# Scans of a hybrid recurrent layer: the next chunk's level matrices earlier, read-outs side by side, the second attention in two parts, the pairs behind the fourth level

## The reference, cut to what matters

```python
def step(S, inp):                       # RWKV-7, 6 heads of 64, one token after the other
    r_t, w_t, kk_t, a_t, v_t, k_t = inp
    sa = jnp.einsum('dbhij,dbhj->dbhi', S, -kk_t)
    S = S * w_t[..., None, :] + sa[..., None] * (kk_t * a_t)[..., None, :] + v_t[..., None] * k_t[..., None, :]
    return S, jnp.einsum('dbhij,dbhj->dbhi', S, r_t)

def step(S, inp):                       # GLA, 4 heads, chunks of 64 tokens
    qc, kc, vc, lac = inp
    b = jnp.cumsum(lac, axis=2)
    diff = b[:, :, :, None] - b[:, :, None, :]
    dec = jnp.exp(jnp.where(mask, diff, -jnp.inf))
    att = jnp.einsum('dbthk,dbshk,dbtshk->dbhts', qc, kc, dec)
    o = jnp.einsum('dbhts,dbshv->dbthv', att, vc) + jnp.einsum('dbthk,dbhkv->dbthv', qc * jnp.exp(b), S)
    bl = b[:, :, -1]
    S = S * jnp.exp(bl)[..., None] + jnp.einsum('dbshk,dbshv->dbhkv', kc * jnp.exp(bl[:, :, None] - b), vc)
    return S, o
```

## Time and profile before

| | |
|---|---|
| runs | 3509.75, 3511.60, 3511.67 us; median 3511.6 |
| profiled execution | 3508.28 us, its span 3506.5 us |
| busy share of the span | PE 90%, DVE 65%, ACT 46%, POOL 25% |
| stage of the scans, 965.0 to 1772.2 us | 807.2 us; PE busy 761.0, DVE 633.4, ACT 386.7, POOL 509.0 |
| one chunk, 1403.04 to 1426.02 us | 22.98 us; PE busy 21.90, DVE 18.48, ACT 11.31, POOL 15.08 |

### The profile page before, as it was taken

How to read it: one execution, slowest core, us unless ns; L and a number is a source line. 1 busy time by engine, 2 the same in 40 slices (tenths; PEclk the granted TensorE clock), 3 DMA queues, 4 the chain that set the end, 5 groups by cost and what they waited for, 6 DMA issues and landing times. The chain is left out here.

```text
span 3506.5 us, 90832 instructions
## 1 busy us (share of the span) xinstructions
PE 3151.4 (90%) x37105; PEld 2875.5 (82%) x37105; DVE 2283.7 (65%) x4484; ACT 1617.0 (46%) x2917; POOL 873.0 (25%) x1232
## 2 busy tenths in 40 slices
PE   7899989999689999999959981799999999999996
PEld 3887867777489889999947760699999999999996
DVE  4575549995478778778867768455555555555555
ACT  2313756665445445444446540344444444444454
POOL 0110000000066666666622200111121111111213
PEclk8999999999799999999979985799999999999998
DMA  5465336665644554444356632565566555655685
GB/s 177 126 182 172 85 99 197 201 201 156 179 109 103 130 135 102 107 106 98 79 155 193 179 105 96 170 194 181 182 200 203 188 189 185 193 181 184 205 291 186
DMA packets 583428, 561.43 MB, mean 160 GB/s; under 512 B 211550, under 2 KB 527262, under 8 KB 582138
## 3 DMA queue, kind: packets, MB, share of 16 engines
q1 hardware_dynamic: 547084, 447.27, 42.7%
q0 software_dynamic: 36016, 109.52, 10.6%
HBM read 418.33 MB, written 138.33 MB: 159 GB/s over the span
## 5 line engine op out<-in xcount | busy, mean ns | idle before, releaser
L3431 DVE TENSOR_TENSOR exp_wlo<-exp_raw,exp_whi 128x2048 fp32r<-128x2048 f32 x192 | 440.0, 2293 | 364.1 <-ACT exp_whi L3332 356.5
L3332 ACT CAST exp_whi<-exp_raw 128x2048 fp32r<-128x2048 f32 x189 | 360.1, 1905 | 75.0 <-DMA exp_raw<-in_w_up 73.5
L1030 PE MATMUL mix_acc<-proj_hThi,mix_wlo 128*128 128x448 f32 (+3 forms) x920 | 357.8, 389 | 14.5 <-DVE mix_wlo L1398 14.5
L1030 PE MATMUL mix_acc<-proj_hTlo,mix_whi 128*128 128x448 f32 (+3 forms) x920 | 335.9, 365 | 0.0
L1030 PE MATMUL mix_acc<-proj_hThi,mix_whi 128*128 128x448 f32 (+3 forms) x920 | 335.7, 365 | 0.0
L3261 PE MATMUL moe_o<-moe_hidhi,exp_wlo 128*128 128x272 f32 x1024 | 308.3, 301 | 2.6 <-DVE moe_hidlo L3545 2.6
L3261 PE MATMUL moe_g<-moe_xThi,exp_wlo 128*128 128x272 f32 x1024 | 300.4, 293 | 1.0 <-DVE moe_xTlo L3435 1.0
L3261 PE MATMUL moe_o<-moe_hidhi,exp_whi 128*128 128x272 f32 x1024 | 298.4, 291 | 0.0
L3261 PE MATMUL moe_g<-moe_xThi,exp_whi 128*128 128x272 f32 x1024 | 297.6, 291 | 0.0
L3261 PE MATMUL moe_u<-moe_xThi,exp_wlo 128*128 128x272 f32 x1024 | 297.1, 290 | 0.0
L3261 PE MATMUL moe_u<-moe_xThi,exp_whi 128*128 128x272 f32 x1024 | 296.9, 290 | 0.0
(11 more groups left out here) (391 smaller groups left out, 8557.9 us busy)
## 6 DMA issues: line engine op xcount, KB each, us to landing
exp_raw<-in_w_gate SPq DMA_DIRECT2D x64, 1024.0 KB, 5.1
exp_raw<-in_w_up SPq DMA_DIRECT2D x64, 1024.0 KB, 5.1
exp_raw<-in_w_down SPq DMA_DIRECT2D x64, 1024.0 KB, 5.1
scn_plain<-rec SPq DMA_DIRECT2D x68, 384.0 KB, 3.6
rec<-mix_arena SPq DMA_DIRECT2D x24, 896.0 KB, 4.3
proj<-mix_out POOLq DMA_DIRECT2D x88, 224.0 KB, 2.5
scn_grc<-grec SPq DMA_DIRECT2D x136, 128.0 KB, 3.7
mix_arena<-in_w_ada SPq DMA_DIRECT2D x12, 1024.0 KB, 6.3
```

The lines of the kernel that those rows point to most:

```text
L1030: mm = pe.matmul(acc[n % ACCS][0:width, 0:tn], wt[:, k, 0:width], hT[hp][:, k, t0:t0 + tn], start=k == 0 and i == 0, stop=k == KD - 1 and ...
L3332: act.copy(w[k % RING][0][:, :, :], raw[k % RAW][:, :, :]).then_inc(hi_done[k % RING], 1)
L3431: dve.tensor_tensor(w[k % RING][1][:, :, :], raw[k % RAW][:, :, :], w[k % RING][0][:, :, :], ALU.subtract).then_inc(lo_done[k % RING], 1)
```

## The change

`attention` gets the range of levels that it is to issue, and `chunk` of PE and of DVE are put in another order. No arithmetic is added or removed. Lines that are the same on both sides are cut.

```diff
-                def attention(g, c):
+                def attention(g, c, levels):
                     u = c % NB
-                    for e in (bk_done if g == 0 else kT_done):
-                        pe.wait_ge(e, c + 1)
-                    if g:
+                    if levels.start == 0:
+                        for e in (bk_done if g == 0 else kT_done):
+                            pe.wait_ge(e, c + 1)
+                        pe.wait_ge(kf_done[g], c + 1)
+                        pe.wait_ge(qf_done[g], c + 1)
+                    if g and levels.stop == NA:
                         pe.wait_ge(lm_done[1], min(c + 2, NCH))
-                    pe.wait_ge(kf_done[g], c + 1)
-                    pe.wait_ge(qf_done[g], c + 1)
-                    for l in range(NA):
+                    for l in levels:
...
# PE, chunk(c)
                     joined(c, 1)
...
+                    if c + 1 < NCH:
+                        strict(c + 1)
                     values_seen(c)
+                    grown(c, 1)
                     read_out(0, c)
-                    grown(c, 1)
                     read_out(1, c)
                     joined(c, 2)
                     state_seen(c)
                     grown(c, 2)
                     keys_by_token(c)
-                    if c + 1 < NCH:
-                        strict(c + 1)
                     joined(c, 3)
                     keys_turned(c)
                     grown(c, 3)
-                    attention(0, c)
+                    attention(0, c, range(NA))
                     joined(c, 4)
+                    attention(1, c, range(CA))
                     grown(c, 4)
-                    attention(1, c)
+                    attention(1, c, range(CA, NA))
                     joined(c, 5)
                     gla_added(0, c)
+                    grown(c, 5)
                     old_state_out(0, c)
-                    grown(c, 5)
                     corrected(0, c)
...
# DVE, chunk(c)
                     joined(c, 1)
...
+                    if more:
+                        strict(0, c + 1)
                     values_seen(0, c)
                     values_seen(1, c)
                     turned(c, 1)
                     read_out(0, c)
                     read_out(1, c)
                     joined(c, 2)
+                    if more:
+                        strict(1, c + 1)
                     turned(c, 2)
                     joined(c, 3)
-                    if more:
-                        strict(0, c + 1)
                     turned(c, 3)
-                    if more:
-                        strict(1, c + 1)
-                        pairs(0, c + 1)
                     joined(c, 4)
+                    attention_masked(0, c)
                     turned(c, 4)
                     if more:
-                        pairs(1, c + 1)
-                    attention_masked(0, c)
+                        pairs(0, c + 1)
                     joined(c, 5)
                     attention_summed(0, c)
+                    if more:
+                        pairs(1, c + 1)
                     attention_masked(1, c)
```

## The result

The changed kernel takes 3551.62 us (median of four runs, 3547.21 to 3556.91), the kernel before in the same comparison 3511.64 (3509.75 to 3513.39): a ratio of 1.0115, 95% interval 1.0099 to 1.0131. The forecast was 3490, 3472 to 3504, with 7 in 100 for slower. It was wrong in sign, and the time lies 48 us above the top of the range.

What follows compares the result with a forecast made beforehand. PE's list, dense but for holes such as 0.93 us before `grown` 4, was taken to bound each scan chunk; 35.3 + 0.3 - 3.9 - 12.4 + 1.5 = 20.8 us saved gave 3490 us, range 3472 to 3504.

Steps and rivals of the forecast that it cites:

- the last stretch on DVE: DVE from the fourth `Ys` to the end of the last masking: 6.73 us where it was 6.35, mask ending at 18.77.
- The slow rival: Early `strict` or its mask slips beyond a 0.3 us margin, delaying the second `joined`: some 3522 us; chance 0.08.
- The holes ahead of `grown` 4 and in front of the mask: PE's 0.93 us wait before level 4's `grown` goes; a new 0.7 us hole comes before the second `old_state_out`.
- 21.9: Length in us forecast for an undisturbed chunk, down from 22.98, 1.07 less.
- The switch to wide loads: PE's read-outs side by side go in and out of 128-column loads once: 0.31 us less per chunk.
- The first chunk: PE's early `strict` waits for the second chunk's load, landing at 973.75: 3.9 us lost.
- The hidden delays of 12.4 us: PE's own holes, formerly hidden in the wait for `Ys` before `grown` 4, now cost 12.4 us; bounds 0 and 12.4.
- 12.4 less 1.5: Cost of newly exposed PE delays, less 1.5 us won back where the new 0.7 hole hides delays before `corrected`.
- The sum of 20.8 us: Total gain over the scans: 35.3 + 0.3 - 3.9 - 12.4 + 1.5 = 20.8 us.
- 35.3 + 0.3 - 3.9: 33 chunks shorter by 1.07 us each, the last chunk's switch gain, less the first chunk's wait for the load.
- The chances: Whole-kernel odds: faster (under 3504.6 us) 0.84, same 0.09, slower 0.07.
- the rivals: Delays stay hidden (3478) 0.22; gain handed back behind level four (3507 to 3515) 0.2; slower 0.08; forecast itself 0.5.

Runs made afterwards that it cites:

- the run with `strict` alone: Kernel before with only strict(c + 1) of PE and DVE moved to the start of the chunk: ratio 0.9970, 3501.1 us.
- the held run: Changed kernel plus one POOL wait: its first large product of group 0 waits for DVE's last sum of the chunk before; ratio 0.9946, 3492.6 us.
- The kernel before with the wait on POOL: Kernel before plus a wait of POOL's first large product of group 0 for DVE's last sum of the chunk before: ratio 0.9993.

## Why the prediction was wrong, by its steps

- **The step that failed: the last stretch on DVE.** It said that from `Ys` 4 to the masking 6.73 pass, and "state additions of DVE end 0.5 before" the next chunk. Between the two lie the sums of group 1, which I carried over at the 1.41 us that they have in the old order. A duration read from a trace holds as long as the neighbours on the other engines stay. I moved PE's `go_mm` forward by 1.6 (POOL starts on it 20.3 into the old chunk) and the sums by 0.4 only (they start 19.7 into the old chunk, 19.2 into the new), wrote of POOL that it "isn't reordered", and didn't set its timeline beside DVE's. POOL starts on that very signal: in the changed kernel at 18.7 after the chunk's start, `KF` at 19.5, the sums' second instruction at 20.0. The term that was missing is two instructions that stand, 1.5 us each, and 0.2 for the first one, beside POOL's `qe`: the sums take 4.46 us (1420.28 to 1424.74) in place of 1.41, 3.05 more, of which 2.07 reach PE. The forecast had no term at all for PE's wait for `att` ahead of the second GLA output. The slow rival that I priced, a late `strict`, was another mechanism, and the run with `strict` alone shows none of it (0.9970).
- By the Trainium skill (SBUF — State Buffer, SBUF: two separate sides) a DVE instruction with two SBUF inputs and a GpSimd instruction that reads SBUF share one port pair, whichever starts first has it for the whole instruction, and the other "fully blocks". The runs agree: 1.92 in place of 0.42 until `KF` ends, `KF` itself 2.14 in place of 1.81, and nothing lost once POOL is held. It was the rule that spoke against this change, and I hadn't weighed it. For a run of short instructions back to back, the 1.95 us of L2281 is longer than the rule's one instruction, and the measurement decides.
- **The holes ahead of `grown` 4 and in front of the mask: right.** The fourth `joined` starts at 11.84 (11.48 forecast, since the late GLA state holds `values_seen` until 1402.86), the mask is done at 19.2 (18.77), the hole is 0.69 (0.7). Undisturbed chunks of the held run, 21.84 and 21.93, against 21.9.
- **The switch to wide loads: right in size.** Both read-outs side by side take 1.48 (1404.41 to 1405.89), against 1.43 by the forecast's terms (0.61 + 0.61 + 0.21) and two blocks of 0.82 before.
- **The first chunk: 2.49 us, not 3.9.** PE stood there, released by the load's last values. The start of `strict` was at 972.13; the landing was taken from a median.

```profile
972.13 2.83 PE L2040 MATMUL scn_b<-scn_plain 64*64 64x64 f32 x48 [2.49 <-DMA scn_Vc<-v_rows]
```

- **The hidden delays of 12.4 us: right in kind, too small in size, as far as the runs tell.** They do come out once the hole is gone: the held run has 27.6 us of visible holes where the kernel before had 15.6, 12.0 more. (The kernel before with the wait on POOL, on the held run's chip, has 22.8, so part of the 12.0 differs from chip to chip.) The times say more. Leaving the loads out wins 38 us on the held run and 15 on the kernel before: by the ratios the loads, and the delays with them, cost the new order 23 us more than the old one (14 to 32 by their intervals), where the forecast had 12.4 less 1.5.
- **The sum of 20.8 us: met in part by luck.** The held run, the forecast's kernel with one wait more, wins 18.9 by its ratio (13.3 to 24.2). But without the loads the new order wins 42 us (0.9837 against 0.9957; 35 to 49), where the forecast's other terms, 35.3 + 0.3 - 3.9, give 31.7. So the gain and the delays were both put too low, and the two misses nearly cancel. (The chances don't quite add up either: by the rivals they are 0.82, 0.10 and 0.08 for faster, same and slower, where 0.84, 0.09 and 0.07 were given.)

## What to carry to other kernels

When an instruction of DVE with two SBUF inputs is moved, or the signal on which POOL starts, lay the two engines' timelines over each other in the new order before taking durations from the old one. If the large POOL instruction has time to spare, make it wait for DVE's sums, or cut it up. And a wait of one engine may be hiding another's delays: before counting it as gain, compare its total with its longest times its count.

## What was not expected of the hardware

A DVE sum of 0.29 us can take 1.8 us beside a POOL product, while the state additions, which have a PSUM input, keep their 1.24 for six. Seven short instructions of POOL in a row held an instruction of DVE until the last was over, 1.95 us, where six short products let DVE in between. One wait of 2 us on PE can cost another 1.15 us, when the granted clock falls behind it. And PE's holes in which it waits for nothing hang on SP's loads: 27.6 us with them, 3.7 without.
